# Old states as moving operand of zero-padded 32-column strips, norm weights at the eviction of gathered columns, and a re-ordered stretch ahead of the experts

## The reference

```python
def step(S, xs):                       # gated DeltaNet, 4 heads, S is 128x128 for each head
    u_c, w_c, qk_c, qg_c, kd_c, gl_c = xs
    v_new = u_c - einsum('bhld,bhdv->bhlv', w_c, S)
    o_c = einsum('bhld,bhdv->bhlv', qg_c, S) + einsum('bhij,bhjv->bhiv', qk_c, v_new)
    S = S * gl_c[..., None, None] + einsum('bhld,bhlv->bhdv', kd_c, v_new)
...                                    # mLSTM, 4 heads, C is 64x128 and n is 64 for each head
num = e_inter[..., None] * einsum('bhld,bhdv->bhlv', q_c, C) + einsum('bhij,bhjv->bhiv', s, v_c)
den = e_inter * einsum('bhld,bhd->bhl', q_c, n) + s.sum(axis=-1)
...
mix = concatenate([_merge(o_a), _merge(h_b)], axis=-1)
x = x + mix @ w_out
xn = _rms(x, norm_moe_g)               # the norm weights are a vector of 1024
logits = xn @ router_w + router_b      # top 4 of 32 experts for each token
...                                    # each expert: clamped SwiGLU, 1024 -> 2x1024 -> 1024
x = x + moe(xn)
x = x + sigmoid(_rms(x, norm_ple_g) @ ple_gate_w) * (p @ ple_w)
y = _rms(x, final_norm_g)
```

## Time and profile before

| | |
|---|---|
| median of 3 runs | 1375.9 us |
| time of the profiled execution | 1375.53 us |
| its span | 1373.8 us |
| mean granted TensorE clock | 0.969 |
| PE busy | 1319.0 us (96%) |
| DVE, ACT, POOL busy | 516.9, 215.7, 54.4 us |
| DMA | 438.81 MB, mean 319 GB/s |
| `gather(0)` starts | 383.11 us |
| expert 0 starts | 390.71 us |

### The profile page before, as it was taken

The page is one execution under the profiler, slowest core; times in us unless marked ns, Lnnn a source line. Parts: engine busy times, 40 slices in busy tenths (PEclk is TensorE's granted clock), DMA queues, the critical chain, the costliest instruction groups (busy, mean ns, idle before and its releaser), DMA issues.

```text
span 1373.8 us, 16930 instructions
## 1 busy us (share of the span) xinstructions
PE 1319.0 (96%) x6236; PEld 584.1 (43%) x6236; DVE 516.9 (38%) x1127; ACT 215.7 (16%) x432; POOL 54.4 (4%) x103
## 2 busy tenths in 40 slices
PE   6999999888999999999999999999999999999997
PEld 5765687663633333333333333333333333333332
DVE  2583445744463322333223332233332233322233
ACT  2350001022021111111111111111111111111112
POOL 5100001000200000000000000000000000000000
PEclk8999999869599999999999999999999999999999
DMA  8231111221679999999999999999999999999941
GB/s 259 75 123 62 62 62 50 90 77 57 256 263 426 428 430 429 428 427 428 427 427 429 428 429 429 428 428 428 428 428 429 429 429 427 428 428 428 429 164 38
DMA packets 55988, 438.81 MB, mean 319 GB/s; under 512 B 12058, under 2 KB 19367, under 8 KB 31354
## 3 DMA queue, kind: packets, MB, share of 16 engines
q1 hardware_dynamic: 55962, 438.45, 77.0%
HBM read 433.41 MB, written 5.02 MB: 319 GB/s over the span
## 4 chain that ended last, share of the span: by engine, by line
PE 77%; DMA 16%; DVE 4%; issue 1%; ACT 1%; SPq 1%; POOLq 0%; POOL 0%; ACTq 0%; DVEq 0%
PE bank L1094 26%; DMA ring<-in_expert_w_gu 16%; PE bank L1105 12%; PE bank L587 8%; PE bank L1050 5%; PE bank L1080 4%; PE bank L1199 2%; PE bank L1115 2%; PE bank L757 2%; PE bank L585 2%; PE bank L1058 1%; PE bank L929 1%; PE bank L800 1%; PE bank L666 1%; PE bank L678 1%
## 5 line engine op out<-in xcount | busy, mean ns | idle before, releaser
L1094 PE MATMUL bank<-ring,SC 128*64 128x512 f32 x2048 | 474.0, 599 | 3.1 <-ACT va L1382 0.7
L1094 PEld LDWEIGHTS bank<-ring,SC 128*64 128x64 f32 x2048 | 136.3, 136 | 288.7 <-issue 257.1
L1105 PE MATMUL bank<-ring,SC 128*64 128x512 f32 x1024 | 226.8, 595 | 0.0
L2021 DVE TENSOR_TENSOR SC<-bank,bgu 128x256 f32<-128x256 f32 x128 | 48.1, 418 | 372.3 <-PE bank L1115 372.3
L1105 PEld LDWEIGHTS bank<-ring,SC 128*64 128x64 f32 x1024 | 70.6, 137 | 133.3 <-issue 127.6
L587 PE MATMUL bank<-xT,ring 128*128 128x320 f32 x384 | 114.2, 445 | 4.7 <-ACTq L1291 3.7
L2008 DVE TENSOR_TENSOR X<-X,bank 128x512 f32<-128x512 f32 x120 | 76.9, 682 | 49.8 <-PE bank L1080 49.8
L1050 PE MATMUL bank<-XS,SC 128*64 128x512 f32 x396 | 90.6, 592 | 0.7 <-issue 0.7
L1391 ACT ACTIVATE SC<-bank 128x512 f32<-128x512 f32 x33 | 19.7, 598 | 453.0 <-PE bank L1050 453.0
L587 PEld LDWEIGHTS bank<-xT,ring 128*128 128x128 f32 x384 | 71.7, 194 | 33.6 <-ACTq L1291 5.6
L2012 DVE TENSOR_TENSOR X<-X,bank 64x256 f32<-64x256 f32 x120 | 50.1, 418 | 92.2 <-PE bank L1083 90.5
(11 more groups left out here) (465 smaller groups left out, 1111.2 us busy)
## 6 DMA issues: line engine op xcount, KB each, us to landing
ring<-in_expert_w_gu SPq DMA_DIRECT2D x128, 2048.0 KB, 20.0
ring<-in_expert_w_down SPq DMA_DIRECT2D x64, 2048.0 KB, 20.9
ring<-in_w_in SPq DMA_DIRECT2D x7, 2048.0 KB, 7.7
ring<-in_w_out SPq DMA_DIRECT2D x2, 2048.0 KB, 8.4
ring<-in_ple_gate_w SPq DMA_DIRECT2D x4, 1024.0 KB, 14.8
out_gdn_s<-ring SPq DMA_DIRECT2D x1, 2048.0 KB, 9.4
X<-in_x_prompt SPq DMA_DIRECT2D x2, 512.0 KB, 3.7
SC<-in_ple_w SPq DMA_DIRECT2D x1, 1024.0 KB, 5.0
```

The lines of the kernel that those rows point to most:

```text
L1094: last = mm(PB[j][SL * h:SL * h + SL, :], xg[:, c % 4, c // 4, :], w[:, FF * h + 512 * j:FF * h + 512 * j + 512], start=(c == 0), stop=(c ...
L1105: last = mm(PB[4][SL * h:SL * h + SL, :], act_t[:, 2 * (c - NGU) + kk, :], w[:, D * kk + 512 * h:D * kk + 512 * h + 512], start=(c == NGU ...
L2021: ins = V.tensor_tensor(out[:, 4 * i:4 * i + 4, :], PB[2 + i][:, :].rearrange("p (k h s) -> p k h s", k=4, h=2)[:, :, h, :], bgu[:, c0 + 4 ...
```

## The change

- **Old states.** A buffer `strips` of 12 groups of 280 columns is laid over the ring's first 3360 columns. ScalarE zeroes it between two projections and copies q of the DeltaNet and q of the mLSTM of the sample tokens into it, 8 columns in every 32; VectorE copies w there instead of into B_WT. A slice of 32 columns of a group, taken at the right offset, holds the 8 tokens of one sequence at their place among four sequences, and zeros for the other three. Now the strip is stationary (32 columns) and the old state moves past it (128 or 129 columns); four sequences accumulate into one bank, and the results come out untransposed. Gone are the two staging copies, `turn_state_sample`, `m_old_state(2)`, and the product with `inds`.
- **Slots 0 and 1** are no longer loaded at 242.66 us, since the strips lie there, but together with slots 2 and 3 after the old states are read. The conv rows are stored earlier, ahead of a projection's weights.
- **Norm weights.** XS is now a plain copy of X by ScalarE. norm_moe_g is read as `gmoe` (128x2x4), and VectorE multiplies by it in a new `take_gathered`, which replaces ScalarE's.
- **Order.** On VectorE the normalised DeltaNet output of t = 2 goes ahead of `m_out(2)`. On TensorE the turns of p move up, the turns of X and the three router products are mixed with the updates of the states, and `ple_part(0)` moves behind the positions. `m_spread` writes to SC (`vexp_m`). The new n goes through a small tile `nrow`, and slots 6 and 7 wait for the store of C alone.

```diff
@@ gdn_state_sample
-                both = PB[3][:, :].rearrange("p (x h s i) -> p x h s i", x=2, h=H, s=NSEQ)
                 for h in range(H):
-                    for s in range(NSEQ):
-                        c = 256 + LS * s
-                        last = mm(both[:, :, h, s, :], S[:, s, h, :], qkv[:, h:h + 5:4, c:c + LS], start=True, stop=True)
+                    for j in range(4):
+                        for x in range(2):
+                            for g in range(2):
+                                i = 4 * g + j
+                                last = mm(PB[3][64 * x + 32 * g:64 * x + 32 * g + 32, P * h:P * h + P], strip(H * x + h, i), S[:, i, h, :],
+                                          start=(j == 0), stop=(j == 3), skip_group_check=True)
@@ m_old_state_sample
+                pe.wait_ge(sem("strips"), 2)
+                pe.wait_ge(sem("wT"), 2)
                 for q in range(2):
+                    for j in range(4):
+                        for hh in range(2):
+                            for g in range(2):
+                                i = 4 * g + j
+                                last = mm(PB[1][64 * hh + 32 * g:64 * hh + 32 * g + 32, 129 * q:129 * q + 129],
+                                          strip(2 * H + 2 * q + hh, i), Cs[:, i, q, :], start=(j == 0), stop=(j == 3),
...
@@ scalar, between the projections
+                if 18 <= j <= 21:
+                    ins = A(strips[:, 3 * (j - 18):3 * (j - 17), :].rearrange("p g c -> p (g c)"), ones[:, 0:1].to_broadcast([P, 3 * 280]),
+                            ACT.Copy, scale=0.0)
...
@@ scalar, before the experts
+            act.wait_ge(sem("dS_ps"), 2 + H)
+            for t in range(3):
+                A(XS[0:ROWS[t], t, :], X[0:ROWS[t], t, :], ACT.Copy).then_inc(sem("XN"), 1)
@@ vector
+            def take_gathered(b):
+                dve.wait_ge(sem("xg_ps"), b + 1)
+                tell(V.tensor_tensor(xg, PB[7][:, :].rearrange("p (j h s) -> p j h s", j=4, h=2),
+                                     bc(gmoe[:, :, :].rearrange("p h j -> p j h"), 3, SL), ALU.mult), "xg")
...
             select(0)
             expert(0, 0)
+            take_gathered(0)
...
             dve.wait_ge(sem("routed"), ROUTED["tables"])
+            take_gathered(1)
             expert(1, 1)
@@ sync
-            sp.wait_ge(sem("C_stored"), 32)
+            sp.wait_ge(sem("C_stored"), 16)
             for c in range(6, 8, 2):
                 load_pair(sp, 0, c)
+            sp.dma_start(o["n_s"].rearrange("o s (q h) (k u) -> (h k) (o s q) u", h=2, u=1),
+                         nrow[:, :, :].rearrange("p s (q u) -> p (s q) u", u=1), allow_slow_non_contiguous=True)\
+                .then_inc(sem("out"), 16)
```

More of the change, by code:

```diff
@@ L159, in build @@
         scf = SC[:, :, :].rearrange("p b x -> p (b x)")
+        vexp_m = [scf[0:64, i * NSEQ * 129:(i + 1) * NSEQ * 129].rearrange("p (s v) -> p s v", s=NSEQ) for i in range(2)]
         def buf(i):
@@ L332, in _ @@
             sp.wait_ge(sem("p_stored"), 48)
-            sp.wait_ge(sem("wqST_ps"), 1)
-            for c in range(2, 4, 2):
+            sp.wait_ge(sem("wqS_ps"), 2)
+            for c in range(0, 4, 2):
                 load_pair(sp, 0, c)
-            sp.wait_ge(sem("qC_ps"), 2)
-            sp.dma_start(mgain, a["norm_moe_g"].to_broadcast([P, D])).then_inc(sem("mgain_in"), 16)
             sp.wait_ge(sem("mix"), 6)
@@ L839, in gdn_turn @@
                 for h in range(H):
-                    last = turn(bank(1, P, h, R), B_ON[t][0:R, h, :], ident[0:R, 0:R])
+                    last = turn(bank(1 if t < 2 else 3, P, h, R), B_ON[t][0:R, h, :], ident[0:R, 0:R])
                 last.then_inc(sem("mixT_ps"), 1)
@@ L895, in m_old_state @@
                 pe.wait_ge(sem("kw"), t + 1)
-                if t == 1:
-                    pe.wait_ge(sem("Cp_done"), 1)
-                    for h in range(H):
-                        last = mm(PB[5 + h // 2][:, 129 * (h % 2):129 * (h % 2) + 129], qm[:, h, P:2 * P], Cp[:, h // 2, :],
-                                  start=True, stop=True)
-                else:
-                    for h in range(H):
-                        last = turn(bank(5, 64, h, P), qC_stage[:, 64 * h:64 * h + 64], ident[:])
+                pe.wait_ge(sem("Cp_done"), 1)
+                for h in range(H):
+                    last = mm(PB[5 + h // 2][:, 129 * (h % 2):129 * (h % 2) + 129], qm[:, h, P:2 * P], Cp[:, h // 2, :],
+                              start=True, stop=True)
                 last.then_inc(sem("qC_ps"), 1)
@@ L1041, in _ @@
             last.then_inc(sem("turned"), 1)
+            ple_part(0)
             pe.wait_ge(sem("pw"), 2)
@@ L1428, in _ @@
             ple_out(2)
-            take_gathered(0)
             expert(0, 0)
@@ L1704, in gdn_take_u @@
                     dve.wait_ge(sem("wT_ps"), t)
-                    tell(V.tensor_copy(B_WT[t][:, :, 0:R], ps(2, P, R)), "wT")
+                    if t == 1:
+                        tell(V.tensor_copy(B_WT[t][:, :, 0:R], ps(2, P, R)), "wT")
+                    else:
+                        dve.wait_ge(sem("strips"), 1)
+                        tell(V.tensor_copy(strip_rows(H), ps(2, P, R).rearrange("p h (s i) -> p h s i", i=LS)), "wT")
             def gdn_values(t):
@@ L1965, in _ @@
             tell(V.tensor_tensor(M_, GT, EQ, ALU.add), "routed")
+            m_add(0)
             m_add(1)
+            dve.wait_ge(sem("Cs_done"), 2)
+            tell(V.tensor_copy(nrow[:, :, :], Cs[:, :, :, DK]), "Cs_done")
             dve.wait_ge(sem("routed"), ROUTED["member"])
@@ L2049, in expert @@
                         add_y(b - 2, t)
+                if age >= 1:
+                    take_gathered(b + 1)
             V.nop().then_inc(sem("x2"), 1)
```

221 lines of the change are left out of this document (101 added, 120 removed).

## The result

The changed kernel takes 1355.33 us, the median of 4 runs (1354.64 to 1356.39), beside 1376.47 us for the kernel before on the same chip (4 runs). The ratio is 0.9847, 95% interval 0.9835 to 0.9859: faster by 21.1 us, where 20.2 were forecast, to 1355.3. The profiled execution took 1356.39 us, with a span of 1354.6 and a mean granted clock of 0.984 (before: 1375.53, 1373.8 and 0.969). All ratios here are those on record; they leave out one slow run of the kernel before (1545.99 us at a granted clock of 0.837) and are not exactly the quotients of the medians beside them.

A forecast was written before the change was run, and what follows sets the result against it. The end was taken as a saturated stream of expert loads behind expert 0's start, so only time before it counts. Terms -7.5 - 4.5 - 9.4 + 1.2 = -20.2 took 1375.5 to 1355.3 us; eight-in-ten range 1343 to 1367.

The forecast's parts named there:

- a. old states read: Reading the old states: 192 strip records at 74 ns, 14.2 us in place of 21.7, -7.5 us (-16.3 to +6.7).
- b. to the first update: Old states to end of w_out of block 0: turns go, a 1.4 us wait comes, 0 (-1.7 to +1).
- c. to the end of w_out of block 1: From the first state update: 21.5 us in place of 26.0, the 4.17 us wait shortened, -4.5 (-5 to -3).
- d. to the gather: End of w_out of block 1 to gather(0), 54.95 us before: 45.5, clock falling partway, -9.4 (-16.2 to -4.8).
- e. gather to expert 0: From gather(0) to expert 0: 7.6 us unchanged, GpSimd's products with mgain being off the path, 0.
- f. expert 1 and the rest: Ahead of expert 1: take_gathered(1) ends after TensorE wants it, and expert 2's first load hangs on it, +1.2 (0 to +2).
- g. early: Fills, copies, conv stores and slot loads, and work in the loop: all fit into gaps, 0 (-0.5 to +2).
- The frame: The end is a fixed stream of 31 experts behind expert 1's first load; time won before expert 0 counts fully.
- the rival on the clock: Clock stays up from w_out of block 1 to the gather: -16.2 in place of -9.4 there, 1346.8 us total; chance 0.16.
- Strips at 148 or 111 ns: Two rivals for the old states: 148 ns a record, 1369.5 us, chance 0.10; not side by side, 1383.7 us, chance 0.06.
- The stream late: Slots 6 and 7 or expert 1's loads land late, giving back 3 to 6 us: about 1360 us; chance 0.08.

The follow-up runs named there:

- strips alone: The kernel before with only the strips for the old states (and what they need), order and norm weights as before: 1358.74 us, ratio 0.9874.
- first wait filled: Changed kernel with two more parts of w_out ahead of the second gdn_o, to fill the 1.33 us wait: 1349.07 us, ratio 0.9803.
- gathered gates: Changed kernel with take_gathered(1) moved ahead of the last product and sum of the expert tables on VectorE: 1351.3 us, ratio 0.9822.
- per-layer product early: Changed kernel with ple_part(0) moved from behind the router of block 1 to ahead of the turns of block 1's rows: 1351.56 us, ratio 0.9827.
- one product more: Changed kernel with one more, unread matrix product of 512 columns in each of 30 expert blocks of the loop: 1373.95 us, ratio 0.998.
- products of S twice: Changed kernel with the strip products of the first kind of state done twice, 128 records more, same result: 1358.05 us, ratio 0.9874.
- output late: Changed kernel with block 2's DeltaNet output normalised behind m_out(2) again, one edit undone: 1352.12 us, ratio 0.9833.
- all filled: Changed kernel with two more w_out parts ahead of the second gdn_o and three ahead of the next wait: 1344.23 us, ratio 0.9762.
- all filled, gathered gates: Changed kernel with all three waits filled with w_out parts and take_gathered(1) ahead of the last table product: 1342.59 us, ratio 0.9753.
- all three edits: Changed kernel with the waits filled, take_gathered(1) ahead of the last table product, and ple_part(0) ahead of the routers: 1341.81 us, ratio 0.9750.
- norm weights alone: The kernel before with only the norm weights moved to VectorE's take_gathered, XS a plain ScalarE copy, GpSimd's products gone: 1378.85 us, ratio 1.0016.

## Why the prediction was right, point by point

The same marks in both profiles, by the prediction's letters (us):

| | forecast | measured | |
|---|---|---|---|
| a. old states read | -7.5 | 7.9 - 21.7 = -13.8 | mis-sized by 6.3 |
| b. to the first update | 0 | (292.60 - 275.76) - 13.1 = +3.7 | wait as forecast, clock not |
| c. to the end of w_out of block 1 | -4.5 | (317.32 - 292.60) - 26.0 = -1.3 | waits as forecast, clock not |
| d. to the gather | -9.4 | (362.68 - 317.32) - 54.95 = -9.6 | right |
| e. gather to expert 0 | 0 | 7.7 - 7.6 = +0.1 | right |
| f. expert 1 and the rest | +1.2 | 984.2 - 983.1 = +1.1 | right |
| g. early | 0 | 267.85 - 267.40 = +0.45 | in range |
| sum | -20.2 | -19.3; the spans differ by -19.2 | |

The frame held: expert 0 moved by 20.3 us, its loads by 20.3, and the loop kept its 28.81 and 29.36. The total, though, is nearer than its terms were, and that was luck: 6.3 us too little in a. and 6.9 too much in b. and c. cancelled. The terms b. and c. lie outside their own ranges (at most +1 and -3), and the strips' 192 records fell below the 11 to 18 us that the prediction named as its sign.

**a.** The price of 74 ns a record, taken from four 64x64 tiles with 256 moving columns, was nearly twice too high: 7.9 us for 192 records is 41 ns each. The strips take 31 ns each once the clock is up (82 in 2.59 us) and 52 to 57 at the start (64 in 3.3 to 3.67). The lower bound of the prediction, a quarter of the 111 ns of the earlier trace rows, 28 ns, was nearly reached. The halving that I had left out "since the clock is at the low level" is what was there, and the clock came up in the middle of the strips, at 271.0 us. That 192 such records were bound by 62 ns each, the rule of the Trainium skill that the prediction weighed (TensorE: Matmul & The Clock Gate, on 56 and 53.3 ns), did not come true: it gave 11.9 us, and 7.9 were measured. Counted for each float32 matmul of the program, which is two records, 31 ns a record would be just 62; no run here tells whether that is what bounds them. The same page of the Trainium skill, on the measured speedup of packing, has 2.38 times for three column tiles of 32; no run here has three, and four give 111 / 31 = 3.6 times, taken as time for a record.

**b. and c.** The waits were forecast at about 1.4 for values, then 0.9 and some 0.9 more in a chain; they are 1.33, 1.01 and 0.67. What was left out is the low clock that comes with short waits. And the wait of 1.33 was of the change's own making: with three parts of w_out ahead of `gdn_o(2)`, as in the strips alone and with the first wait filled, the way from the strips to the first update takes 10.2 us in both profiles, where the changed kernel with one part takes 16.8. The prediction said of the rival on the clock that "no idle above 1.5 us is left", as if a shorter one were harmless. The kernels speak against that. Low granted clock between the strips and the end of w_out of block 1, from the clock's records of each profile, the waits there, and the time from the strips to expert 0:

| kernel | waits left, us | low early | low late | strips to expert 0 | by the clock's sum |
|---|---|---|---|---|---|
| changed, first profile | 1.33, 1.01, 0.67 | 17.1 | 17.1 | 102.5 | (the base) |
| changed, second | the same | 17.1 | 17.1 | 102.4 | 102.5 |
| gathered gates | the same | 6.8 | 23.9 | 100.6 | 100.8 |
| per-layer product early | the same | 6.8 | 17.1 | 96.4 | 96.7 |
| one product more | the same | 6.8 | 23.9 | 101.0 | 100.8 |
| products of S twice | the same | 3.4 | 17.1 | 100.5 | 100.2 |
| output late | 1.33, 3.94 | 6.8 | 13.7 | 97.5 | 98.0 |
| first wait filled | 1.01, 0.68 | 3.4 | 17.1 | 93.9 | 94.4 |
| all filled | none | 0 | 17.1 | 90.5 | 91.0 |
| all filled, gathered gates | none | 0 | 23.9 | 92.8 | 94.4 |
| all three edits | none | 0 | 17.1 | 89.2 | 90.3 |

The last column is worked out: 102.5, less half of each microsecond of low clock that went (an mLSTM update, L911, takes 3.69 us at the full level and 7.25 at the low one, about twice as long), less the waits that went, the 0.69 for ScalarE's eviction where the per-layer product moved among them, and plus 4.5 for the doubled products (12.4 - 7.9 us for all strips). It comes within 1.6 us everywhere, and within 0.6 in eight of ten. So this stretch is described well by two things, its waits and its low clock. In eight profiles with some of these waits there is low clock early; in the three without them there is none, though a wait of 0.67 for X, between the blocks of w_out, is left in those too. That supports the waits as the cause; it isn't a proof, since filling them also moves dense work. Nor is a wait enough: a fall followed the wait of 1.33 in five of the seven profiles that have it, and the two of 1.01 and 0.67 in four of seven. In five profiles TensorE's order up to the end of w_out is the same to the instruction (the changed kernel twice, gathered gates, per-layer product early, one product more), and they lost 17.1, 17.1, 6.8, 6.8 and 6.8 us there. Why is open: nothing was run that sets where in time a wait falls and changes nothing else. By the sum above the three waits cost their own 3.0 and 1.7 to 8.5 for the clock, as the build happens to fall.

The same kind of chance lies ahead of the strips. The program there is the same in the changed kernel and all its variants, yet the first L853 starts at 266.12 to 269.97 us. The clock's records differ there too: six of these eleven profiles have 3.4 us at the full level near 20 us, and eight have a low stretch of 3.4 us near 160. So differences of up to 4 us between two totals need not come from the edit, and term g., 0.45, is within that.

The same page of the Trainium skill, on a second failure mode of the clock, tells of a kernel in which TensorE stops briefly between groups of matmuls, often enough that the clock goes back and forth; the trace agrees, with stops of 0.67 to 1.33 us.

**d.** 45.5 forecast for "a fall partway through", 45.4 measured: the clock fell near 340, in the routers, and came back near 357, in the per-layer products. Here the forecast chose between two bounds and met the middle; that none of the three early waits is needed for this fall is shown by the kernels that have them filled and fall too, with TensorE busy for 17.00 of 17 us. It was neither the clock up all through (38.7) nor low all through (50.1). Which of the router's products, the turns and the updates brings the fall was not taken apart. Moving the per-layer product only changed which product pays.

**The rivals.** Clock up through d.: no. Strips at 148 or 111 ns: no, 31 at the full level and 52 to 57 at the low one. The stream late: no, the load for expert 1 leaves when expert 0 allows it, and the loop shows no new wait. What is left is a wait of 1.04 us for L1996, forecast at 1.2, and taking it away gave it back (1.1 us on average). Of the whole gain, 18.1 us are the strips; the norm weights alone cost 2.1. The mixing of turns, routers and updates was not run alone, and the order on VectorE only by taking it back, which cost nothing that can be told; by subtraction the two bring some 5 to 8 us together, with the loss in b. in it.

## What to carry to other kernels

Here the matmuls with 16 moving columns and 128 stationary ones took 219 ns each, with the weight loads busy for 14.78 of 15.00 us. Turned round, with the narrow operand padded to 32 stationary columns, they ran four side by side at 31 ns, and the clock rose within their stream. A wait of TensorE, even one of 1 us, should be priced with the low clock that may come with it: here filling 3.0 us of waits, by moving products from behind to ahead of them and saving no work, won 8.2 us in one set of runs and 11.1 against the changed kernel's first time. When two builds differ by a few us, compare the granted clock of each stretch before reading anything into the order of instructions.

## What the runs showed that I had not expected

- 32-column strips with 128 moving columns take 31 ns a record at the full clock (90 in 2.78 us), four side by side; 16 moving columns on 128 stationary ones took 219 at the low clock.
- Those 16-column matmuls kept TensorE busy at 0.50 from 275 to 290; in the changed kernel the clock rises within the strips, at 271.
- The same changed kernel, in two sets of four runs: 1355.33 and 1352.4 us, with a single run at 1346.59, while the median of the kernel before stayed at 1376.4 to 1376.8 in all sets.
- VectorE's products of 128x96 take 0.25 us alone and 1.26 and 1.79 beside GpSimd's products of 128x1024.
